# The first layer of the cache compression with tokens instead of head dimensions on the partitions, fed from a copy of the cache pages laid out anew in DRAM

## What is computed

```python
def compress_kv(kv, pe, w1, w2):          # kv: (B, L, 2 heads, key/value, 128)
    nc = L // NSA_BLOCK                    # blocks of 64 tokens
    blk = kv[:, :nc * NSA_BLOCK].reshape(B, nc, NSA_BLOCK, NSA_KV_HEADS, 2, HEAD_DIM)
    blk = blk + pe[None, None, :, None]
    flat = blk.transpose(0, 1, 3, 4, 2, 5).reshape(B, nc, NSA_KV_HEADS, 2, NSA_BLOCK * HEAD_DIM)
    hid = jax.nn.silu(jnp.einsum('bngcf,cfe->bngce', flat, w1))
    return jnp.einsum('bngce,ced->bngcd', hid, w2)
...
    past_cmp = cache_cmp_kv[layer, page_table].reshape(B, past, NSA_KV_HEADS, 2, HEAD_DIM)
```

## Time and profile before

| | |
|---|---|
| median of 3 runs | 2949.38 us (2940.37 to 2951.59) |
| profiled execution | span 2961.1 us from its first to its last instruction |
| TensorE busy | 95% of the span |
| VectorE, ScalarE, GpSimd busy | 77%, 47%, 12% |
| mean granted TensorE clock | 0.974 |
| DMA | 440.20 MB, 149 GB/s |

### The profile page before, as it was taken

One profiled execution on the slowest core, in us unless ns is written; L12 is line 12 of the kernel. 1 busy time (PEld: TensorE's weight loads), 2 busy tenths in 40 slices (PEclk: granted clock), 3 DMA queues, 4 the chain that ended last, 5 costly groups with the idle time before them and its releaser, 6 DMA issues.

```text
span 2961.1 us, 55633 instructions
## 1 busy us (share of the span) xinstructions
PE 2816.4 (95%) x22709; PEld 2694.5 (91%) x22709; DVE 2273.6 (77%) x3546; ACT 1391.7 (47%) x2383; POOL 345.4 (12%) x322
## 2 busy tenths in 40 slices
PE   8999999999989878989989999999999999999998
PEld 8999999988878657889989999999999999999997
DVE  6656777877657667755588888888888888888898
ACT  5434455555546544532254444444444454434345
POOL 0010000014270215123320000000000000000002
PEclk9999999999979988999999999999999999999998
DMA  7564443458631883663353435343444464534342
GB/s 221 178 205 110 122 128 109 116 183 283 237 134 52 327 241 107 167 175 87 86 172 112 140 102 141 112 139 107 135 122 130 116 208 155 161 115 145 123 143 99
DMA packets 521999, 440.20 MB, mean 149 GB/s; under 512 B 36270, under 2 KB 476773, under 8 KB 515665
## 3 DMA queue, kind: packets, MB, share of 16 engines
q1 hardware_dynamic: 457906, 303.50, 35.6%
q0 software_dynamic: 19568, 80.16, 7.4%
q10 hardware_dynamic: 44272, 52.98, 5.3%
HBM read 378.33 MB, written 66.55 MB: 150 GB/s over the span
## 4 chain that ended last, share of the span: by engine, by line
PE 49%; DVE 4%; ACT 1%; issue 1%; DMA 1%; POOL 0%; ACTq 0%; POOLq 0%; DVEq 0%
PE i L3373 42%; PE i L140 7%; DVE f_half L3930 1%; DVE x_blocks L3968 1%; DMA x_blocks<-s_blk 0%; DVE h_rows L3963 0%; DMA s_h<-resid 0%; DVE x_blocks L3896 0%; ACT resid L3556 0%; DVE w_ring L3919 0%; ACT x_blocks L3695 0%; DVE ln_parts L3974 0%; PE i L3383 0%; ACT x_blocks L3570 0%; DVE f_sum L3923 0%
## 5 line engine op out<-in xcount | busy, mean ns | idle before, releaser
L3373 PE MATMUL i<-x_blocks,f_half 128*128 128x272 f32 x10752 | 1361.1, 288 | 24.6 <-DVE h_rows L3963 10.7
L3373 PEld LDWEIGHTS i<-x_blocks,f_half 128*128 128x128 f32 x10752 | 1351.4, 189 | 29.9 <-DVE x_blocks L3968 13.9
L570 PE MATMUL a<-xb_in,w_half 128*128 128x272 f32 x4200 | 545.3, 291 | 8.4 <-DVE w_half L972 4.5
L570 PEld LDWEIGHTS a<-xb_in,w_half 128*128 128x128 f32 x4200 | 534.7, 189 | 17.4 <-issue 7.2
L3623 ACT CAST f_half<-w_ring 128x1024 fp32r<-128x1024 f32 (+2 forms) x370 | 346.3, 936 | 403.9 <-PE i L3373 340.4
L3930 DVE TENSOR_TENSOR f_half<-w_ring,f_half 128x1024 fp32r<-128x1024 f32 (+2 forms) x362 | 392.6, 1084 | 81.3 <-ACT f_half L3623 78.9
L3930 DVE TENSOR_TENSOR f_half<-f_sum,f_half 128x1024 fp32r<-128x1024 f32 (+2 forms) x148 | 159.4, 1077 | 80.8 <-ACT f_half L3623 80.6
L972 DVE TENSOR_TENSOR w_half<-w_ring,w_half 128x1024 fp32r<-128x1024 f32 x129 | 157.4, 1221 | 78.6 <-ACT w_half L708 78.3
L3623 ACT CAST f_half<-f_sum 128x1024 fp32r<-128x1024 f32 (+2 forms) x148 | 138.7, 937 | 150.0 <-PE i L3373 150.0
L708 ACT CAST w_half<-w_ring 128x1024 fp32r<-128x1024 f32 x125 | 131.3, 1051 | 109.4 <-PE a L570 105.7
L3336 POOL TENSOR_TENSOR f_half<-w_ring,f_half 128x512 fp32r<-128x512 f32 x8 | 12.6, 1570 | 1400.8 <-ACT f_half L3623 1400.8
(11 more groups left out here) (595 smaller groups left out, 4202.2 us busy)
## 6 DMA issues: line engine op xcount, KB each, us to landing
w_ring<-in_ffn_w_up_dram SPq DMA_DIRECT2D x88, 1024.0 KB
w_ring<-in_w_in_dram SPq DMA_DIRECT2D x52, 1024.0 KB, 8.8
w_ring<-in_ffn_w_down_dram SPq DMA_DIRECT2D x24, 1536.0 KB, 7.6
w_ring<-in_w_o_dram SPq DMA_DIRECT2D x16, 1024.0 KB
x_blocks<-s_blk ACTq DMA_DIRECT2D x17, 816.0 KB, 5.8
s_proj<-st ACTq DMA_DIRECT2D x48, 272.0 KB, 2.7
s_blk<-x_sums ACTq DMA_DIRECT2D x22, 544.0 KB, 6.6
kv_ring<-in_cmp_w_dram SPq DMA_DIRECT2D x16, 512.0 KB, 6.9
```

The source lines that it names most:

```text
L570: last = nc.tensor.matmul(ps[bank][:, 0:HT2], half(q, w)[:, k], XB[v[j]][:, k], start=j in (0, 1, 3) and k == 0 and i == 0, stop=k == HK - ...
L3373: last = nc.tensor.matmul(ps[bank][:, 0:HT2], half(e, j, wl_)[:, s], XB[:, x0 + s, xl_, BLK_OF[j]], start=start and s == 0 and i == 0, sto ...
```

## The change

The program copies the pages into a new DRAM tensor `s_cmp` with another order of dimensions, and compresses from that copy.

1. In the input projection, after the weight loads of pair e, for e from 4 to 22, SP issues the copies of 7 pages (`cached_page`): it loads the page number into a register and issues two DMAs (`by_token`), one for each block of 64 tokens. In a copy the run that stays contiguous is 32 floats, 128 bytes: 64 tokens x 4 (head, key/value) x 4 quarters, 1024 runs a DMA, from DRAM to DRAM. There are 256 of these, 8 like them for the prompt's blocks, and 8 small ones for `pe` (256 runs each).
2. `s_cmp` is read as `token_rows`: partitions are (half h of the head dimension, token), 2 x 64, and a partition's row is 266 blocks (256 cached, 8 of the prompt, 2 columns that hold `pe`) of 32 dimensions. There are 8 such units k (key/value, quarter, head). Each is loaded by two DMAs, one for partitions 0 to 63 and one for 64 to 127, of 34048 bytes a partition; three places are used in turn. `w1` comes in 16 pieces, each in two DMAs of 64 partitions as well.
3. The gathers and transposes, the separate work on the prompt and the addition of `pe` go. ScalarE copies four of the 32 dimensions at a time to a high part (64 copies of 128x1064) and VectorE makes the low part. TensorE does 64 x 12 = 768 products of 266 columns, whose moving operand takes every fourth float. The product of the `pe` column is added as the bias of the Silu.
4. The second layer of the keys is done in the middle of the stage (`keys`), when the values' products run.

```diff
+                def by_token(block, src):
+                    sp.dma_start(S_cmp[:, :, :, block].rearrange("q t k e -> t k q e"),
+                                 src.rearrange("t g c (q e) -> t (g c) q e", q=4)).then_inc(cmp_out, 16)
+
+                def cached_page(i):
+                    page = nc.sync.value_load(PTS[i // 8:i // 8 + 1, i % 8:i % 8 + 1], min_val=0, max_val=NPOOL - 1)
+                    src = A["cache_cmp_kv"][0, bass.ds(page, 1)]
+                    for n in range(2):
+                        by_token(2 * i + n, src[:, n * BLK:(n + 1) * BLK].rearrange("o t g c d -> (o t) g c d"))
...
+                    if 4 <= e < 23:
+                        for i in range(7 * (e - 4), min(7 * (e - 3), B * NPG)):
+                            cached_page(i)
...
+        def rows_load(eng, k, a, b):
+            c, q, g = k // 4, (k // 2) % 2, k % 2
+            for h in range(2):
+                eng.dma_start(XC[k % 3][h * BLK:(h + 1) * BLK, a:b], S_cmp[2 * h + q, :, 2 * g + c, a:b]).then_inc(xc_in[k], 16)
+
+        def w1_load(eng, i):
+            c, d0 = i // 8, (i % 8) * 8
+            for h in range(2):
+                eng.dma_start(W1R[raw_place(i)][h * BLK:(h + 1) * BLK], W1v[c][h][:, d0:d0 + 8]).then_inc(w1_in[i], 16)
...
+                sp.wait_ge(cmp_out, 32 * (B * NPG + QT) + 16 * 4 * KVH)
+                sp.wait_ge(mq, job(NP_IN - 1, 0) + 1)
+                rows_load(sp, 0, 136, NCC)
+                sp.wait_ge(mq, job(NP_IN - 1, 1) + 1)
+                for i in range(3):
+                    w1_load(sp, i)
                 sp.wait_ge(mq, job(NP_IN - 1, 2) + 1)
-                w1_load(sp, 0)
+                w1_load(sp, 3)
+                sp.wait_ge(mq, job(NP_IN - 1, 3) + 1)
+                rows_load(sp, 0, 0, 136)
...
-                gp.wait_ge(mq, job(NP_IN - 1, 0) + 1)
-                for u in range(AHEAD):
-                    gather(gp, u)
...
+                rows_load(sp, 1, 0, NCC)
                 sp.dma_start(W2[:], A["cmp_w2"][0].rearrange("c e d -> e c d")).then_inc(w2_in, 16)
+                for i in (4, 5, 6, 7):
+                    raw_again(i)
+                sp.wait_ge(wls, 3)
+                sp.wait_ge(tails_out, 32)
+                rows_load(sp, 2, 0, NCC)
+                rows_again(3)
+                for i in (8, 9, 10):
+                    raw_again(i)
+                rows_again(4)
+                raw_again(11)
+                rows_again(5)
...
+                for u in range(ALL):
+                    k, m = u // NT, u % NT
+                    n, g, c = k // 2, k % 2, k // 4
...
+                    pe.wait_ge(xl, u + 1)
+                    for d in range(4):
+                        wh, wl = WH[n > 0][:, 4 * m + d], WL[:, 4 * m + d]
+                        x, y = XH[u % 4][:, :, d], XL[u % 4][:, :, d]
+                        for i, (a, b) in enumerate(((wh, x), (wh, y), (wl, x))):
+                            last = nc.tensor.matmul(ps[4 + 2 * c + g][:, 0:NCC], a, b, start=k % 4 < 2 and m == 0 and d == 0 and i == 0,
+                                                    stop=k % 4 > 1 and m == NT - 1 and d == 3 and i == 2)
                     last.then_inc(used, 1)
```

More of the change, by code:

```diff
@@ L228, in w1_load @@
-        def w1_load(sp, i):
-            for c in range(2):
-                sp.dma_start(W1[:, c, i * 8:(i + 1) * 8], W1v[c][:, i * 8:(i + 1) * 8]).then_inc(w1c[i], 16)
         ahead = list(held)
@@ L1191, in build, with w_tiles, old_done @@
[L1191 removed]
+            ALL = NU * NT
+            w2_in, xh, xl, whs, wl0, wls, used, pb, hid, out4, ckv = (
+                sem("c_" + n) for n in ("w2_in", "x_hi", "x_lo", "w_hi", "w_lo_first", "w_lo", "used", "pe_sum", "hid", "out", "ckv"))
             block = ph.enter_context(nc.Block())
+            def w_tiles(area, i):
+                return area[:, (i % NPC) * 8:(i % NPC + 1) * 8]
+            def old_done(i):
+                return 2 * NT * (i // NPC) - NT + 2 * (i % NPC) + 2
@@ L1194, in _, with raw_again @@
             @block.sync
             def _(sp):
-                for i in range(1, 8):
-                    if i >= 2:
-                        sp.wait_ge(trd, 16 * (i - 2) + 2)
-                    if i == 2:
-                        sp.wait_ge(tails_out, 32)
-                        rows_stored(sp)
+                def raw_again(i):
+                    before = i - 4 if i < 7 else i - 3
+                    if before == 0:
+                        sp.wait_ge(wl0, 1)
+                    else:
+                        sp.wait_ge(wls, before)
@@ new lines, in hidden @@
+                def hidden(c):
+                    act.wait_ge(pb, c + 1)
+                    for g in range(KVH):
+                        acc = ps[4 + 2 * c + g]
+                        nc.scalar.activation(HID[:, c, g * 256:(g + 1) * 256], acc[:, 0:256], ACT.Silu, bias=PEB[:, c:c + 1])
+                        if c == 0:
+                            last = nc.scalar.activation(HIDP[:, :, g], acc[:, 256:256 + NPB], ACT.Silu, bias=PEB[:, 0:1])
+                        else:
+                            last = nc.scalar.activation(HIDX[:, g], acc[:, 256:256 + NPB].rearrange("p (o n) -> p o n", o=1).broadcast_to((P, GRP, NPB)), ACT.Silu, bias=PEB[:, 1:2])
+                    last.then_inc(hid, 1 + c)
@@ L1323, in _, with pe_sum @@
+                for u in range(ALL):
+                    if u < NT and u % 2 == 0:
+                        w_hi(u // 2)
+                    x_hi(u)
+                    if u == 3:
+                        rows_stored(act)
+                    for i in range(NPC, 2 * NU):
+                        if u == old_done(i) + 3:
+                            w_hi(i)
+                    if u == ALL // 2 + 4:
+                        hidden(0)
+                hidden(1)
             @block.vector
             def _(dve):
-                def prompt(q):
-                    dve.wait_ge(pr_ps, q + 1)
-                    for c in range(2):
-                        src = ps[6 + q % 2][:, :].rearrange("p (g c n t) -> p c t n g", g=KVH, c=2, n=2)[:, c]
-                        dst = XPT[:, c, :, 4 * q:4 * q + 4].rearrange("p t (n g) -> p t n g", n=2)
-                        for n in range(2):
-                            last = nc.vector.tensor_tensor(dst[:, :, n], src[:, :, n], PET[:, c].rearrange("p (t o) -> p t o", o=1).broadcast_to((P, BLK, KVH)), ALU.add)
-                    last.then_inc(pr_t, 1)
+                def pe_sum(c):
+                    dve.wait_ge(used, (c + 1) * ALL // 2)
+                    nc.vector.tensor_copy(PEB[:, c:c + 1], ps[4 + 2 * c][:, NCC - 2:NCC - 1]).then_inc(pb, 1)
```

249 lines of the change are left out of this document (102 added, 147 removed).

## The result

The changed kernel takes 3009.27 us (median of four executions, 3003.84 to 3011.82), the kernel before 2947.6 beside it: a ratio of 1.0209, 95% interval [1.0189, 1.023], 61.7 us more. The forecast said 2985 us, 36 more: the right side and inside the range, but 24 us too low.

A forecast was written before the change was run, and what follows sets the result against it. TensorE, busy 95% of the span, was taken to bound the kernel; the new stage would wait for loads. +28 us for the stage and +8 us for page copies on 2949.4 gave 2985 us, range 2915 to 3120 (8 in 10).

The forecast's parts named there:

- The start of the loads: Compression stage: the first unit's load may be issued at 623.0 us and lands at 653.3, against 652.7 for products now.
- the copies' 8 us: Projection: page copies fill the DMA queue, so TensorE stalls twice on late weight loads, +8 us over the whole.
- rival 2: Page copies in the projection: 128-byte DRAM writes are dear, 20 to 31.9 ns a packet, total 3080 to 3270 us; 18%.
- It just fits, without reserve: Projection: a pair's page copies plus other DMA work need 22.2 us, against the pair's 22.1 us on TensorE.
- 213 GB/s for loads by halves: Loads of `token_rows` and `w1`: DMAs over 64 partitions get half of 426 GB/s.
- Rival 1: Stage loads: the two half-partition DMAs run together at up to 426 GB/s, stage ends 62 us earlier, total 2887 to 2895; 17%.
- 8 units and 16 pieces, 43.25 MB: Compression stage: all bytes counted for the loads, so the last unit is there at 826.1 us.
- TensorE computes a unit in 12.4 us: Compression stage: products at 128.7 ns, units arriving each 20 to 28 us, so TensorE idles about half the time.
- the forecast's end, 858.1: End of the compression stage: 849.1 us against 822.5 now, plus 1 for the clock and 8 for the page copies.
- Rival 3: Stage products: the strided operand costs 1.02 ns a column, 26 us a unit; stage ends at some 884, total 3018; 10%.
- The saving reckoned for the arithmetic: Compression stage, loads apart: engines need about 101 us where the loop now takes 157.

## Why the prediction came out as it did

**The start of the loads and the copies' 8 us: right in size, by luck, for the cause is another.** The projection's last products stand at 651.90 where they stood at 643.84, and the first unit is issued at 630.85, as 623.0 + 8 says. No pair waits for `w_ring`: from 300 to 640 us TensorE is as busy as before. The forecast had counted two stalls of TensorE on late weight loads. The loss lies at 150 to 300 us (138.77 us busy, 143.97 before). TensorE's waits there, after:

```profile
PE a L619 <- DVE w_half L1018: 4.6, 2, 4.2
PE a L647 <- DMA raw_rows<-in_gdn_conv_w_dram: 4.3, 1, 4.3
PE a L647 <- DMA raw_rows<-in_ffn_conv_w_dram: 2.3, 1, 2.3
```

Before, the three were 3.8, 0.5 and 1.7 us. So 4.4 us more are waits for GpSimd's small loads of `raw_rows`, which come late while the page copies fill the DMA engines, and 0.8 are for `w_half`. The rest, some 3 us, goes with a clock of 0.93 in place of 1.00 from 200 to 250. The experiment with fewer copies shows the first of these. The price of a packet: (0.94 - 0.44) x 22.1 us x 16 / 14336 = 12.3 ns, forecast 13.9; rival 2 falls. "It just fits, without reserve" agrees with eight pages a pair, which did not fit, though their 22 us are not explained by the price.

**213 GB/s for loads by halves: right, the exact figure by luck.** The mean is 213 GB/s (46.07 MB); with all engines busy it is 226, and the hole in SP's list takes the difference. Rival 1, halves that do not cost, falls by that and by the single DMA's 356 GB/s. The Trainium skill, "SBUF — State Buffer", section "Door 1: The DMA port swizzle", gives 196 GB/s for 64 partitions at 1 MiB. The trace has the mean 9% above that; whether the ports of the partitions are the reason, as the page says, no run here shows apart from the number of DMAs.

**"8 units and 16 pieces, 43.25 MB": 13 us too little.** The last unit was due at 826.1 + 8 = 834.1 and came at 847.1. In this time 2.8 MB more than these were moved, and 2.8 MB at 213 GB/s are 13 us. 1.1 MB went by ScalarE's queue, another 1.6 by SP's, whose list also has stores of 0.3 MB, the second layer's weights, constants and, from 813.3 us on, the queries of attention (2 MB, `mix`). The forecast counted no bytes but the units and pieces.

**"TensorE computes a unit in 12.4 us": the step that failed.** It is 23.2 us (96 x 242 ns): the rate was taken from products that read neighbours, and these read every fourth float. So TensorE does not idle half of the time, and has no gap in the windows at 680, 740 and 780 us. Behind the last load this costs 25.5 us in place of 12.4 + 2 and 1 for the clock, 10 us. The 13 and the 10 are the distance from the forecast's end, 858.1 (849.1 + 1 + 8), to the measured 881.2. Rival 3, at 10%, had the mechanism: not its 26 us but near, and its total, 3018 us, came closer than my 2985. Its end of 884 I can't get again from its terms: 653.3 + 2 + 768 x 271 ns + 8.6 are 872, with 8 for the copies 880. That this is near 881.2 is in part luck, for its unit is too slow by 3 us and it has none of the gaps (15 us at 716 and the late start, 669.3 in place of 663).

**What the forecast did not see.** It is right by its number and its side, and wrong in half of its mechanism. It named the loads as the limit and the strided operand as an alternative, when both held at once. Removed one by one they give 10 and 21 us, together 84. The saving reckoned for the arithmetic (157 to 101 us) was not reached by any kernel here that computes the whole stage: the turn from dimensions-last to blocks-last is paid for by TensorE (242 ns) or by ScalarE and VectorE (2.1 us a copy), and the best of them equals the kernel before. What is left open is how far that one would come with SP's list in another order.

## What to carry to other kernels

A layout that saves transposes moves the turn elsewhere: look at what each engine then reads float by float, and price it with a kernel that reads neighbours, before trusting the product count. Load over all 128 partitions by one DMA, and look at its outermost dimension on both sides: with 128 all DMA engines were busy, with 2 only two. Where two limits lie close, test each alone and both together: the small gain of one alone says nothing on its worth.

## What was not expected of the hardware

- An fp32r product of 266 columns, 8 or 16 bytes apart, takes 237 to 242 ns, against 124 for neighbours at a granted clock of 1.00. With 16 bytes it is the same 242 at 669 to 672 us, at a clock of 0.50 of 2.4 GHz, where neighbours take 221: the reading sets it, not the clock.
- A copy of 128x1064 floats in single floats takes 2.0 to 2.2 us on ScalarE and VectorE, whether source or destination is apart; in pieces of two floats 1.18 and 1.27 us.
- One DMA with an outermost dimension of 2 ran on two engines at 52 GB/s in all, and held everything behind it on the queue.
- Packets of 128 bytes from DRAM to DRAM cost some 12 ns of one DMA engine here, below the 13.9 ns of the line through the rows of before, so with no sign of a further price for short writes.
- GpSimd's work beside VectorE's two-operand subtractions slowed both: from 2081 to 2519 ns on VectorE as a mean (up to 4075 for one), from 2.3 to 4.0 us on GpSimd.
